# Expert arms of a mixture layer: one loop over seven groups, and a native fp32 piece for 129 to 192 rows

## The reference, cut to what matters

```
logits = h @ w_router;  top_logit, top_e = top_k(logits, 2);  gates = softmax(top_logit)
for each expert e, for its rows x:   y = (silu(x @ w1[e]) * (x @ w3[e])) @ w2[e]
out = layer_norm(alpha * x + g2 * sum over the token's two experts of gate * y)
```

## Time and profile before

| what | value |
|---|---|
| median of three runs | 2327.46 us |
| span of the profiled execution | 2325.5 us |
| its own time as a run | not listed apart; the three runs are 2327.46, 2328.38, 2322.58 |
| TensorE matmul busy | 2242.9 us (96%) |
| VectorE busy | 1504.3 us (65%) |
| ScalarE busy | 1105.1 us (48%) |
| GpSimd busy | 346.4 us (15%) |
| DMA, mean over the span | 220 GB/s |
| chain that ended last | TensorE 90%, VectorE 5%, issue 2%, ScalarE 2%, DMA 1% |

### The profile page before, as it was taken

How to read it: one execution, slowest core, us unless ns; L and a number is a source line. 1 busy time by engine, 2 the same in 40 slices (tenths; PEclk the granted TensorE clock), 3 DMA queues, 4 the chain that set the end, 5 groups by cost and what they waited for, 6 DMA issues and landing times.

```text
span 2325.5 us, 30122 instructions
## 1 busy us (share of the span) xinstructions
PE 2242.9 (96%) x11426; PEld 1840.4 (79%) x11427; DVE 1504.3 (65%) x1370; ACT 1105.1 (48%) x1134; POOL 346.4 (15%) x205
## 2 busy tenths in 40 slices
PE   7999999999999999799999999999999999999994
PEld 5876688888878888687888888888888888888882
DVE  3466667666677444896444544459999995444994
ACT  4145535222225222675434434357777774434772
POOL 0030007999960000000000000000000000000001
PEclk8999999999999998899999999999999999999997
DMA  7490023545432223898454555459999996454883
GB/s 323 182 333 31 4 91 145 199 176 196 188 145 85 97 72 119 347 373 297 183 198 180 200 198 188 191 205 395 366 402 360 401 372 241 180 198 180 325 306 146
DMA packets 76180, 512.76 MB, mean 220 GB/s; under 512 B 8240, under 2 KB 8368, under 8 KB 19024
## 3 DMA queue, kind: packets, MB, share of 16 engines
q1 hardware_dynamic: 61344, 442.46, 49.9%
q0 software_dynamic: 14768, 69.35, 7.9%
HBM read 482.41 MB, written 29.36 MB: 220 GB/s over the span
## 4 chain that ended last, share of the span: by engine, by line
PE 90%; DVE 5%; issue 2%; ACT 2%; DMA 1%; SPq 0%; DVEq 0%; POOL 0%; ACTq 0%; POOLq 0%
PE ps L1768 27%; PE ps L1770 26%; PE ps L1769 26%; PE ps L572 2%; PE ps L527 2%; PE ps L583 2%; PE ps L2165 1%; DVE lo L1137 1%; PE ps L1827 1%; PE ps L531 1%; DVE fl L1441 1%; PE ps L1946 1%; PE ps L2100 0%; DMA raw<-w_mod 0%; DMA raw<-w_pre 0%
## 5 line engine op out<-in xcount | busy, mean ns | idle before, releaser
L1768 PE MATMUL ps<-ah,hi 128*128 128x512 f32 (+1 forms) x768 | 285.1, 371 | 5.6 <-DVE al L1302 2.4
L1770 PE MATMUL ps<-ah,lo 128*128 128x512 f32 (+1 forms) x768 | 283.6, 369 | 0.0
L1769 PE MATMUL ps<-al,hi 128*128 128x512 f32 (+1 forms) x768 | 283.5, 369 | 0.0
L1636 DVE TENSOR_TENSOR he<-se,ps 128x512 f32<-128x512 f32 x112 | 77.0, 687 | 286.2 <-ACT se L1038 286.1
L1385 DVE TENSOR_TENSOR lo<-raw,hi 128x2048 fp32r<-128x2048 f32 x112 | 255.8, 2284 | 0.0
L1768 PE MATMUL ps<-hia,xth 128*128 128x512 f32 x616 | 247.8, 402 | 6.1 <-issue 4.7
L1385 DVE TENSOR_TENSOR loa<-raw,hia 128x2048 fp32r<-128x2048 f32 x112 | 251.1, 2283 | 1.1 <-ACT hia L911 1.1
L1385 DVE TENSOR_TENSOR lob<-raw,hib 128x2048 fp32r<-128x2048 f32 x112 | 251.6, 2283 | 0.0
L1038 ACT ACTIVATE se<-ps 128x512 f32<-128x512 f32 x112 | 67.0, 598 | 382.5 <-PE ps L1770 382.5
L1768 PE MATMUL ps<-hib,xth 128*128 128x512 f32 x616 | 245.7, 399 | 0.0
L1768 PE MATMUL ps<-hi,hh 128*128 128x512 f32 x616 | 240.8, 391 | 2.2 <-DVE hl L1640 1.5
(11 more groups left out here) (275 smaller groups left out, 3983.6 us busy)
## 6 DMA issues: line engine op xcount, KB each, us to landing
raw<-w_moe SPq DMA_DIRECT2D x336, 1024.0 KB, 5.5
raw<-w_pre SPq DMA_DIRECT2D x59, 1024.0 KB, 4.9
raw<-w_mod SPq DMA_DIRECT2D x20, 1024.0 KB, 7.4
raw<-w_mod POOLq DMA_DIRECT2D x14, 1024.0 KB, 5.1
rawm<-w_mod POOLq DMA_DIRECT2D x14, 1024.0 KB, 5.2
dispatched_x<-zt POOLq DMA_DIRECT2D x22, 512.0 KB, 10.8
xg<-dispatched_x POOLq DMA_DIRECT2D x8, 1024.0 KB, 7.4
expert_y<-ys POOLq DMA_DIRECT2D x8, 1024.0 KB, 5.1
```

The costliest lines, as they stand in the source:

```text
L1636: dve.tensor_tensor(HE[:], SE[:], up_view(q, 1), ALU.mult).then_inc(he_ready, 1)
L1768: pe.matmul(outp, wh, ah, start=first, stop=False, skip_group_check=True)
L1769: pe.matmul(outp, wh, al, start=False, stop=False, skip_group_check=True)
L1770: return pe.matmul(outp, wl, ah, start=False, stop=last, skip_group_check=True)
```

## The change

An expert's kind now depends on its rows: up to 128 kind 0 (one tile), 129 to 160 kind 1 (one tile and a piece of 32 rows), 161 to 192 kind 2 (one tile and a piece of 64), above that kind 3 (two tiles). The piece is computed in native fp32 from the raw weights, in strips of 32 or 64 columns of the array. Each strip takes another part of the moving weights and writes other partitions of the bank that the second tile would use.

```diff
+PIECE = 32
+PIECE_MAX = 64
+PIECE_AREA = PIECE + PIECE_MAX
+PIECE_STORES = 6
-        WHERE = {0: (0, 0), 1: (1, 1), 5: (2, 5), 2: (3, 3), 3: (4, 4), 4: (5, 2)}
+        WHERE = {0: (0, 0), 1: (1, 1), 2: (2, 3), 3: (3, 4), 4: (5, 2), 5: (4, 5)}
+        READER = {0: 0, 1: 0, 2: 1, 3: 1, 4: 2, 5: 3}
...
+        def store_pieces(eng, i, stored):
+            one = yg_d[bass.ds(i * PIECE_AREA + PIECE_ROWS, PIECE), :]
+            two = yg_d[bass.ds(i * PIECE_AREA + (PIECE_ROWS + PIECE), PIECE_MAX), :]
+            for c in range(4):
+                eng.dma_start(one[:, c * 256:(c + 1) * 256],
+                              YS[c * PIECE:(c + 1) * PIECE, 1, 0:256]).then_inc(stored, 16)
+            for c in range(2):
+                eng.dma_start(two[:, c * 512:(c + 1) * 512],
+                              YS[c * PIECE_MAX:(c + 1) * PIECE_MAX, 1, 0:512]).then_inc(stored, 16)
...
 (SP)
+                def after_piece(j, src):
+                    slot = WHERE[j][0]
+                    sp.wait_ge(raw_used[slot], t.n(("raw", slot)))
+                    if read is not None:
+                        sp.wait_ge(piece_read[READER[j]], read[0] if j == 5 else read[1])
+                    sp.dma_start(RAW[slot][:], src).then_inc(raw_loaded[slot], 16)
...
             with t.loop(sp, NE * GROUPS - 1, RAW_TURN) as g:
-                next_units(g * 6)
+                now = sp.value_load(TT[0:1, bass.ds(g, 1)], min_val=1, max_val=NE * GROUPS + 1)
+                then = sp.value_load(TT[0:1, bass.ds(g + 1, 1)], min_val=1, max_val=NE * GROUPS + 1)
+                next_units(g * 6, (now, then))
             load(WHERE[5][0], unit((NE * GROUPS - 1) * 6 + 5))
+            sp.wait_ge(ys_b, NE + 1)
+            store_pieces(sp, NE - 1, last_pieces)
...
 (POOL, store; the gather then takes its rows from BACK instead of DI)
+                if pieces:
+                    store_pieces(pool, i, y_out)
...
 (ScalarE; token_tiles has the same with XTF)
             def hidden(q):
-                act.activation(HH[:].rearrange("p a n -> p (a n)"), PS[:, 2 * q, :], ACT.Copy).then_inc(hh_ready, 1)
+                act.activation(HH[:].rearrange("p a n -> p (a n)"), PS[:, 2 * q, :], ACT.Copy)
+                act.activation(HF[:], PS[:, 2 * q, :].rearrange("p (k n) -> p k n", k=2)[:, :, P:P + PIECE_MAX],
+                               ACT.Copy).then_inc(hh_ready, 1)
...
 (VectorE, before routed: 14 instructions, of which 10 are waited for, in the place of one; 7 after it)
-            step(dve.tensor_copy(RI[:, 0:12], RF[:, 0:12]))
+            dve.tensor_scalar(PIECED[:], counts, float(P), None, ALU.is_gt)
+            dve.tensor_scalar(BEFORE[:], counts, float(P + PIECE), None, ALU.is_gt)
...
 (TensorE)
+            def piece_up(q, m):
+                outs = PS[:, 2 * q + 1, :].rearrange("p (a n) -> p a n", a=2)
+                wide = 2 * m
+                for k in range(KD):
+                    for j in range(P // m):
+                        ins = pe.matmul(outs[m * j:m * (j + 1), :, 0:wide], XTF[:, k, 0:m],
+                                        RAWU[q][:, :, k, wide * j:wide * (j + 1)], start=(k == 0), stop=(k == KD - 1),
+                                        skip_group_check=True, tile_position=(0, m * j))
+                ins.then_inc(piece_read[q], 1)
...
+            def piece_down(q, m):
+                w = RAW[WHERE[4 + q][0]][:].rearrange("p (k n) -> p k n", k=2)
+                wide = 8 * m
+                for k in range(2):
+                    for c in range(P // m):
+                        ins = pe.matmul(PS[m * c:m * (c + 1), 6, 0:wide], HF[:, k, 0:m], w[:, k, wide * c:wide * (c + 1)],
+                                        start=False, stop=True, skip_group_check=True, tile_position=(0, m * c))
+                ins.then_inc(piece_read[2 + q], 1)
...
+            def expert(tiles, r, more, m=0):
...
+                with t.loop(pe, GROUPS, turn) as g:
+                    up_first(tiles, r, m)
+                    with pe.If(g > 0):
+                        down(1, tiles, m)
+                        turn_hidden(0, tiles, m)
+                    up_second(tiles, g, m)
+                    with pe.If(g < 1):
+                        pe.wait_ge(ys_a, r)
+                        pe.wait_ge(ys_b, r)
+                        for b in range(4 if m or tiles == 2 else 2):
+                            pe.matmul(PS[:, 4 + b, 0:1], ident, BEFORE[:, 0:1], start=True, stop=True, skip_group_check=True)
+                    down(0, tiles, m)
+                    turn_hidden(1, tiles, m)
...
+            def by_count(e, r):
+                kind = pe.value_load(RI[0:1, bass.ds(e, 1)], min_val=0, max_val=3)
+                saved = dict(t.at)
+                with pe.If(kind < 1):
+                    expert(1, r, e < NE - 1)
+                t.at = dict(saved)
+                with pe.If(kind == 1):
+                    expert(1, r, e < NE - 1, PIECE)
...
-            with t.loop(pe, NE - 1, times(turn, GROUPS)) as e:
-                either(e, e + 1, True)
-            either(NE - 1, NE, False)
+            with t.loop(pe, NE, times(turn, GROUPS)) as e:
+                by_count(e, e + 1)
```

More of the change, by code:

```diff
@@ L763, in rows, with store @@
                 return buf[at, :].rearrange("(s p) n -> p s n", p=P)
-            def store(i, n):
+            def store(i, n, pieces):
                 pool.wait_ge(ys_a, n + 1)
@@ L1623, in _ @@
+            for c in range(2):
+                ins = dve.tensor_tensor(OP[:, c], OH[:, c], PB[:], ALU.mult)
+            step(ins)
+            step(dve.tensor_reduce(DF[:], OP[:], AX.X, ALU.add))
+            dve.tensor_copy(BACK[:], DF[:]).then_inc(back_ready, 1)
             dve.wait_ge(gate_exp, 1)
@@ L2146, in up, with up_part, up_first @@
+            def up_part(q, tiles, s, i, k, first, last):
+                hi, lo = ((HIA, LOA), (HIB, LOB))[q]
+                cols_ = slice(s * P, (s + 1) * P)
+                return three(PS[:, 2 * q + s, :], XTH[:, k, cols_], XTL[:, k, cols_], hi[:, :, k, :], lo[:, :, k, :],
+                             first, last)
+            def up_first(tiles, r, m):
+                for j in (0, 1):
                     arrived(j)
-                hi, lo = ((HIA, LOA), (HIB, LOB))[q]
-                ks = [k for i in XT_ORDER for k in (2 * i, 2 * i + 1)] if r is not None else list(range(KD))
+                ks = [k for i in XT_ORDER for k in (2 * i, 2 * i + 1)]
```

175 lines of the change are left out of this document (115 added, 60 removed).

## The result

The changed kernel takes **2246.43 us** (median of 4 runs, 2245.22 to 2246.70) against 2325.75 us for the kernel before (4 runs, 2322.58 to 2328.38): ratio 0.966, 95% interval 0.9645 to 0.9674. It is 79 us faster; 2236.7 was forecast, so the sum was 9.7 us too good, inside its range.

The account below looks back on a forecast made before the run. TensorE was taken as the only bound in two-tile experts. Pieces -103.0, routing +3.2, arms +6.2, clearing matmuls +0.8, tail +2 give -90.8: span 2325.5 to 2234.7, plus 2.0 makes 2236.7 us; range 2215 to 2284.

Parts of the forecast that it names:

- The bound: Two-tile experts: TensorE is the only bound; a second tile costs 116 us, all of it on TensorE.
- The price of a 32-row group: Expert 1's groups: blocks 5.3 us, edges 1.0, transposes 0.3, together 6.6 us a group and 46 for the expert.
- The 64-row group: Expert 6's groups: blocks 10.6 us plus edges and transposes, 11.8 a group and 82 for the expert.
- Who holds what up: Pieced groups: weight waits have 3 to 4 us of cover; one-tile groups: 0.2 us left per half group, cost 0.
- One-tile experts: Group loop: extra copy, register loads and back edge cost 0; clearing matmuls 0.4 us, half covered or more.
- Routing: VectorE's extra small steps, 3.9 us, partly absorbed by an existing TensorE wait: +3.2 us (bounds 2 and 5).
- Between arms: After expert 0, TensorE jumps over three unused arms instead of one, about 3.1 us a jump: +6.2 us.
- Tail: Kernel's end: last pieces' stores on SP's queue and normalisation rows starting later, +2 us (bounds 0 and 4).
- Thin cover: One-tile groups: cover gone on VectorE (+21 us) or through SP's late loads (+52), 2258 to 2289; chance 0.12.
- strips that don't overlap: Pieced groups: strips sharing one set of weights each pay alone, 185 us more, 2422; chance 0.04.
- The arms pushing each other out: TensorE's instruction store: longer loop not kept, 7.3 us at each of 6 later expert changes, 2281; chance 0.17.
- The rival in which no expert takes a piece: Routing: counts come out otherwise, so only the extras stay, about 2333 us; chance 0.01.

Follow-up runs that it names:

- the kernel without pieces: Changed kernel with both piece limits set to 128 rows, so the piece arms stay in the code but are never taken: 2349.64 us.
- strips in a row: Changed kernel with a piece's up block running all eight k of one column strip before the next strip: 2338.6 us.
- 64 rows for expert 1: Changed kernel with the limit between the pieces set to 128 rows, so expert 1 takes the 64-row piece: 2280.91 us.
- blocks together: Changed kernel with both up blocks of a pieced group together, ahead of the last k of the first up projection: 2244.69 us.
- the chain: Changed kernel with its four arms tested as else-ifs, so an expert that ran its arm goes straight to the loop's end: 2248.61 us (one run).
- the reordered chain: Changed kernel with the arms tested as else-ifs and the two-tile arm ahead of the 64-row arm: 2243.75 us.
- the walk: Changed kernel with else-if arms reordered, both up blocks together, and TensorE passing over the arms without entering any while waiting for the first rows: 2237.86 us.
- A walk with three long jumps: Changed kernel with TensorE passing once over all four separately tested arms, entering none, while waiting for expert 0's rows: 2261.01 us.

## Why the prediction held, step by step

- **The bound.** Right. In the pieced experts TensorE has no wait but the one gap and 0.3 us ahead of expert 6's last down part; the one-tile experts wait in their first group only and ahead of the last down part. The two pieced experts carry the saving, and the kernel without pieces is 1% slower than before.
- **The price of a 32-row group, 6.6 us: measured 7.37.** The blocks were nearly right: 1.88 and 1.00 against 1.76 and 0.88, and of the edge of 0.25 per block 0.1 lies in front (1143.45 to 1143.77 instead of 0.23) and 0.1 behind it (1145.65 to 1145.99). Four blocks with their edges come to 6.5 instead of 6.3. The mis-sized term is the piece's **transposes**, 0.3 us a group: each of the two turns takes 0.31 + 0.27 us where a one-tile turn takes 0.13, so 0.88 more. Strip matmuls and full-width ones meet here too.
- **The 64-row group, 11.8 us: measured 12.0** (28.89 against 16.87). The total is right, in part by luck: the blocks take 10.9 instead of 10.6, the transposes 0.4 instead of 0.2, and the edges 0.7 instead of 1.0.
- **Who holds what up.** Right. No wait for a low part or a raw unit inside a pieced group once it runs. ScalarE does wait for its units there, in the slack forecast for it; the units land after 6.7 us in the median, not 5.5, under the 9 us at which they would have set the pace. In the one-tile experts the cover is as forecast, 0.2 us:

```profile
1707.46 0.69 DVE L1719 TENSOR_TENSOR he<-se,ps 128x512 f32<-128x512 f32 x1 [0.23 <-ACT se L1087]
...
1710.57 0.69 DVE L1723 TENSOR_TENSOR hl<-ps,hh 128x512 fp32r<-128x512 f32 x1 [0.22 <-ACT hf L1092]
```

  The wait of 0.40 us in the earlier trace rows is 0.23, and VectorE now waits 0.22 for the new copy. The group still takes 16.87 us.
- **One-tile experts, 0: measured 0.7 each.** The clearing matmuls were hidden as forecast: they push the first group's transposes back, and the wait for the gated product falls from 0.78 to 0.33 us. What was put at nothing and isn't is the back edge of the group loop. The first group is now part of the loop, TensorE has just waited there, and nothing is queued that could cover the back edge. The transposes to the next wide matmul take 0.82 us instead of 0.29:

```profile
1641.24 0.44 PE L2278 MATMUL ps<-small,he 128*128 128x128 f32 x2 [0.33 <-DVE he L1719]
1642.06 0.49 PE L1851 MATMUL ps<-hia,xth 128*128 128x512 f32 x1 [0.38 <-issue]
```

  The other 0.2 us is a wait for VectorE's low part ahead of the last down part. +2.3 us over experts 3 to 5.
- **Routing, +3.2: 2.9 from its own steps**, and the stage began 4.4 us later in this trace, in code that is the same; some 2 us of that lie within the spread of the kernel before (944.57 and 946.65).
- **Between arms, +6.2: measured +6.7**, close for a reason that was not the forecast's. It put 3.1 us to a jump. The one long branch before lasted 6.1 us, of which 3.4 lay under matmuls that were already queued; the three after it took 13.6 in all, under matmuls that covered 3.2.

```profile
L2216 PEldq COMPARE_BRANCH  x8: 72/208/6081, 1069.7 to 2274.6; - x8
```

  So the distance ahead of expert 1 grew by 7.9 us, from 5.0 to 12.9. The half clock behind it cost 1.4 us instead of 2.6, and that is luck of this trace: behind the same three branches it cost 1.5 to 2.9 in four others (the second trace of the changed kernel, strips in a row, 64 rows for expert 1, blocks together). Expert 0 itself was 1.2 us shorter than in the first trace of the kernel before, which began it at half clock, and 0.8 longer than in the second, which did not. What the jumps pay for is code that is not at hand: three places at once here, three in two gaps in the chain (14.3 us), two in the reordered chain (8.6).
- **Tail, +2: not settled.** From the last store on it takes 45.8 us, against 46.0 in the first trace of the kernel before and 42.5 in the second: -0.2 or +3.3. Nothing shows that the six pieces' stores and the later normalisation rows are hidden.
- **Rivals.** Thin cover and strips that don't overlap are refuted by the rows above. The arms pushing each other out did not happen, but it is real: one arm more and it costs not the 44 us worked out for it but 167, since most far jumps pay again and not each change of expert once. The rival in which no expert takes a piece was added up wrongly: by the forecast's own terms it ends at 2327.5 + 3.2 + 6.2 + 0.8 + 2, near 2340 and not 2333; it measured 2349.64.

The sum was 10.4 us too good against the span: 4.5 of it in experts 0 and 1 (5.2 in expert 1's own groups, at 0.77 each for transposes and blocks, 0.5 for the arms, less 1.2), 4.1 ahead of the first token tile, 2.3 in the one-tile experts, 0.8 in expert 6 and 0.3 in expert 2, with 1.6 back from the last. The 1.2, the 4.1 and the 1.6 change with the trace of the kernel before that is taken.

## What to carry to other kernels

Before adding a variant of a loop body, count the instructions of everything that takes turns on that engine: the cost of code is small up to a size, which lies here between some 1,800 and 2,200 instructions (estimates), and then comes back at most jumps, 167 us for an arm that never runs. Below that size the order of the tests still decides which jumps pay, by a rule that these runs don't give. Strips of the array overlap only when neighbours in the stream lie on different strips, so put the strip loop inside. A gap of a few microseconds on TensorE costs more than its length, because a start at half clock follows, and less than its length where it gives another engine time to catch up: so moving a gap may win nothing, and filling a wait that is there anyway (the walk) did.

## What the runs showed that was not expected

- Code that a walk brings in, without running an arm, stays at hand for a while: a walk with one long jump, in a wait of 15 us, removed a gap some 130 us later. It was gone another 170 us later, behind expert 1's arm. A walk with three long jumps cost 14.6 us in all.
- In the chains the jump to the loop's end took 5.7 to 5.9 us behind expert 1, though TensorE had run that code some 175 us before.
- Left open: the fetch rows don't say which engine they serve, so how many blocks TensorE keeps was not counted, and the two loops bound it only for arms tested one after the other.
- With five arms in the loop a branch that had cost 0.2 us cost 4.8, and 46 fetches became 117.
- A native fp32 pass of 128 columns in one 32-column strip takes 0.092 us alone and 0.118 for four strips taking turns.
- A block of strip matmuls has a fixed price of 0.13 to 0.16 us beside 0.2 at its two edges, and putting two side by side saves 0.16 us a group at 32 rows and 0.34 at 64, where 0.17 of it comes from the transposes that a block no longer follows.
- A loop's back edge that costs nothing while TensorE has work queued takes 0.5 us behind a wait that has emptied its queue.
